# Gathered tokens of experts 1 to 15 turned by 32x32 blocks on VectorE, and w_down loaded as whole rows

## The reference, cut to what matters

```python
    tok = h.reshape(T, D)
    logits = (tok @ router_w).astype(jnp.float32)
    aff = jax.nn.softmax(logits, axis=-1)
    cap = max(1, min(T, CAPACITY_FACTOR * T // N_EXPERTS))
    gate, idx = lax.top_k(aff.T, cap)
    xs = tok[idx]
    hid = jax.nn.silu(jnp.einsum('ecd,edf->ecf', xs, w_gate)) * jnp.einsum('ecd,edf->ecf', xs, w_up)
    ye = jnp.einsum('ecf,efd->ecd', hid, w_down) * gate[..., None].astype(h.dtype)
    out = jnp.zeros_like(tok).at[idx.reshape(-1)].add(ye.reshape(-1, D))
```

## Time and profile before

| what | us |
|---|---|
| median of 3 runs (1491.0 to 1491.63) | 1491.59 |
| span of the profiled execution | 1489.4 |
| PE busy | 1467.0 (99%) |
| DVE busy | 1189.5 (80%) |
| ACT busy | 819.8 (55%) |
| POOL busy | 167.3 (11%) |
| slot_tokens_T_lo, 15 times 1024 elements | 18.3 |

### The profile page before, as it was taken

One profiled execution on the slowest core, in us unless ns is written; L12 is line 12 of the kernel. 1 busy time (PEld: TensorE's weight loads), 2 busy tenths in 40 slices (PEclk: granted clock), 3 DMA queues, 4 the chain that ended last, 5 costly groups with the idle time before them and its releaser, 6 DMA issues.

```text
span 1489.4 us, 18913 instructions
## 1 busy us (share of the span) xinstructions
PE 1467.0 (99%) x7042; PEld 1235.5 (83%) x7042; DVE 1189.5 (80%) x1024; ACT 819.8 (55%) x777; POOL 167.3 (11%) x119
## 2 busy tenths in 40 slices
PE   9999999999999999998999999999999999999996
PEld 8878888888888888888888888888888888888885
DVE  5688988896767766346888888888888888888886
ACT  6322232123622222333677777777777777777776
POOL 1000001000005200011110112011110121012101
PEclk9999999999999999999999999999999999999998
DMA  7210232623263255677999999999999999999997
GB/s 236 58 43 0 81 87 75 224 85 99 94 230 121 87 183 197 227 253 283 347 362 365 376 376 374 384 374 377 374 377 381 377 374 374 384 376 376 374 374 286
DMA packets 220971, 388.26 MB, mean 261 GB/s; under 512 B 8603, under 2 KB 87771, under 8 KB 220412
## 3 DMA queue, kind: packets, MB, share of 16 engines
q1 hardware_dynamic: 213692, 361.39, 68.4%
q0 software_dynamic: 7232, 26.22, 5.8%
HBM read 348.78 MB, written 38.80 MB: 260 GB/s over the span
## 4 chain that ended last, share of the span: by engine, by line
PE 71%; DVE 2%; DMA 0%; issue 0%; ACT 0%; POOLq 0%; POOL 0%; ACTq 0%
PE ps L1779 23%; PE ps L1781 22%; PE ps L1780 22%; PE ps L2162 1%; PE ps L2154 1%; PE ps L2199 1%; PE ps L2082 0%; PE ps L2064 0%; DMA slot_tokens<-tok_rows,rows_to_gather 0%; DVE top_index L1651 0%; DVE affinity_rows L1654 0%; DVE top_of_halves L1647 0%; DVE expert_lo L1207 0%; DVE tok_rows L1592 0%; ACT expert_hi L804 0%
## 5 line engine op out<-in xcount | busy, mean ns | idle before, releaser
L1207 DVE TENSOR_TENSOR expert_lo<-expert_raw,expert_hi 128x2048 fp32r<-128x2048 f32 (+1 forms) x285 | 597.5, 2110 | 92.1 <-ACT expert_hi L804 91.1
L804 ACT ACTIVATE expert_hi<-expert_raw 128x2048 fp32r<-128x2048 f32 (+1 forms) x285 | 506.5, 1778 | 177.8 <-PE ps L1781 174.0
L1779 PE MATMUL ps<-expert_hi,slot_tokens_T_hi 128*128 128x512 f32 (+1 forms) x768 | 289.8, 377 | 2.0 <-DVE slot_tokens_T_lo L1207 1.0
L1780 PE MATMUL ps<-expert_lo,slot_tokens_T_hi 128*128 128x512 f32 (+1 forms) x768 | 285.2, 371 | 0.0
L1781 PE MATMUL ps<-expert_hi,slot_tokens_T_lo 128*128 128x512 f32 (+1 forms) x768 | 285.2, 371 | 0.0
L1779 PE MATMUL ps<-hT_hi,w_hi 128*128 128x512 f32 x576 | 226.2, 393 | 1.0 <-DVE hT_lo L1219 1.0
L1781 PE MATMUL ps<-hT_hi,w_lo 128*128 128x512 f32 x576 | 224.3, 389 | 0.0
L1780 PE MATMUL ps<-hT_lo,w_hi 128*128 128x512 f32 x576 | 224.2, 389 | 0.0
L1779 PEld LDWEIGHTS ps<-expert_hi,slot_tokens_T_hi 128*128 128x128 f32 x768 | 144.1, 188 | 25.1 <-issue 4.0
L1781 PEld LDWEIGHTS ps<-expert_hi,slot_tokens_T_lo 128*128 128x128 f32 x768 | 144.2, 188 | 20.4
L1241 DVE SCALAR_TENSOR_TENSOR conv_sum<-a_padded,small_params,conv_sum 128x1024 f32<-128x1024 f32 x120 | 158.1, 1317 | 3.4
(11 more groups left out here) (314 smaller groups left out, 1843.6 us busy)
## 6 DMA issues: line engine op xcount, KB each, us to landing
expert_raw<-in_w_gate SPq DMA_DIRECT2D x64, 1024.0 KB, 8.7
expert_raw<-in_w_up SPq DMA_DIRECT2D x64, 1024.0 KB, 8.6
expert_raw<-in_w_down SPq DMA_DIRECT2D x64, 1024.0 KB, 8.1
expert_raw<-in_w_gate SPq DMA_DIRECT2D x32, 768.0 KB, 7.5
expert_raw<-in_w_up SPq DMA_DIRECT2D x32, 768.0 KB, 7.2
expert_raw<-in_w_down SPq DMA_DIRECT2D x32, 768.0 KB, 8.5
w_raw<-in_w_in SPq DMA_DIRECT2D x36, 512.0 KB, 4.8
gate_in<-gate_spill SPq DMA_DIRECT2D x22, 512.0 KB, 3.9
```

What stands on the lines that cost most here:

```text
L804: nc.scalar.activation(out, src, ACT.Copy, **scale).then_inc(s, 1)
L1207: V.tensor_tensor(out, src, high_part.bitcast(F32), ALU.subtract).then_inc(s, 1)
L1779: nc.tensor.matmul(out, a[0], b[0], start=first, stop=False)
L1780: nc.tensor.matmul(out, a[0], b[1], start=False, stop=False)
```

## The change

**Tokens.** For experts 1 to 15 the 8 transposes on PE are gone. POOL copies four numbers a partition (`pieces_to_gather`) and issues four indirect DMAs, each of 128 pieces of 1 KB: of a token row's four quarters, the one that a partition gets depends on the 32-partition group that it lies in, and on which of the four DMAs it is. DVE then turns XS in place in blocks of 32x32 (`turn_tokens`, one STREAM_TRANSPOSE over 8x128 elements a partition, seen with a step of 8 elements, 32 bytes), right behind the low part of block 12. After it partition p holds, of each token, the channels 8p to 8p+7. So gate and up weights are loaded with 8 adjoining rows to a partition ("(p t)" for "(t p)"), in pieces as long as before. `xsT_high` and `xsT_low` read XS in SBUF with a step of 32 bytes, where they read PSUM with none, and write as before. The gather for expert e+1 is now issued ahead of the scatter of expert e-1, once `xsT_low` of expert e is done. On PE `hidden_T(2)` follows block 17 without a wait, and the wait for `xsT_lo` is behind it. XS of expert 0 is still turned by PE.

**Start.** The numbers of the pieces are made once: four small ACT copies (`slots_four_times`), four small PE transposes (`slot_pieces`), one DVE tensor_scalar and four memsets.

**w_down.** A block is two row tiles of all 1024 columns (pieces of 4 KB in DRAM), where it was all row tiles of 512 columns (2 KB). For chunks 0 and 1 that is 2048 elements as before; for chunk 2 it is 2048 elements and 1024 in place of twice 1536. PE goes through both column halves of a tile before the next tile, and ACT's scaling of the output waits for both blocks.

```diff
@@ -417,16 +423,20 @@
             if kind == "down":
-                tiles = n // P
-                return w_down[bass.ds(e, 1), a:a + n, k * 512:(k + 1) * 512].rearrange(
-                    "o (t p) n -> p (o t) n", p=P), tiles, 512
+                tiles, _ = place_of(kind, c, k)
+                a += 2 * k * P
+                return w_down[bass.ds(e, 1), a:a + tiles * P, :].rearrange("o (t p) n -> p (o t) n", p=P), tiles, D
             w = w_gate if kind == "gate" else w_up
-            return w[bass.ds(e, 1), k * 4 * P:(k + 1) * 4 * P, a:a + n].rearrange(
-                "o (t p) n -> p (o t) n", p=P), 4, n
+            return w[bass.ds(e, 1), :, a:a + n].rearrange(
+                "o (p t) n -> p (o t) n", p=P)[:, 4 * k:4 * k + 4, :], 4, n
 
         def place_of(kind, c, k):
             a, n = FC[c]
-            return (n // P, 512) if kind == "down" else (4, n)
+            return (min(2, n // P - 2 * k), D) if kind == "down" else (4, n)
@@ -740,20 +749,20 @@
             def gather(e):
 
-                if not isinstance(e, int):
-                    pool.wait_ge(xs_in, e * 16)
-                    pool.wait_ge(xsT_mm, e)
-                pool.wait_ge(slots_ready, 2)
-                nc.gpsimd.tensor_copy(NEXT_ROWS[:], SLOTS[:, bass.ds(e, 1)]).then_inc(rows_next, 1)
+                pool.wait_ge(xs_in, (e - 1) * 64 + 16)
+                pool.wait_ge(xsT_lo, e)
+                pool.wait_ge(slots_ready, 5)
+                nc.gpsimd.tensor_copy(NEXT_PIECES[:], PIECES[:, bass.ds(e, 1), :].rearrange("p o a -> p (o a)")).then_inc(rows_next, 1)
 
                 pool.wait_ge(x2_mm, WO_DONE)
                 pool.wait_ge(rows_next, e)
-                pool.indirect_dma_start(XS[:], None, tok_dram,
-                                        bass.IndirectOffsetOnAxis(ap=NEXT_ROWS[:], axis=0)).then_inc(xs_in, 16)
+                for a in range(4):
+                    pool.indirect_dma_start(XS[:, a * 256:(a + 1) * 256], None, tok_pieces,
+                                            bass.IndirectOffsetOnAxis(ap=NEXT_PIECES[:, a:a + 1], axis=0)).then_inc(xs_in, 16)
@@ -772,16 +781,19 @@
             gather(1)
+            gather(2)
             scatter(0)
-            with pool.Fori(1, E - 1) as e:
+            with pool.Fori(2, E - 1) as e:
                 gather(e + 1)
-                scatter(e)
+                scatter(e - 1)
+            scatter(E - 2)
@@ -1108,17 +1120,18 @@
-                act.wait_ge(xsT_mm, e + 1)
-                high(XST[0][:].rearrange("p k n -> p (k n)"), PS[:, 6:8, :].rearrange("p a n -> p (a n)"), xsT_hi)
+                act.wait_ge(xs_turned, e + 1)
+                act.wait_ge(e_used, e * NB - SKIPPED - len(down_units(1)))
+                high(XST[0][:], XS_BY_TILE, xsT_hi)
 
             def gate_out(e, used):
 
                 for dh in range(2):
                     act.wait_ge(slots_ready, 3)
-                    act.wait_ge(e_used, used + dh)
+                    act.wait_ge(e_used, used + 1)
@@ -1132,6 +1145,12 @@
+                    if first and n == 2:
+                        act.wait_ge(pair_ready, 1)
+                        for a in range(4):
+                            part = nc.scalar.activation(FOUR_TIMES[:, a, :, :], PAIR[:, 1, 32 * a:32 * a + 32][:, None, :].to_broadcast([E, 4, P // 4]),
+                                                        ACT.Copy)
+                        part.then_inc(rows_ready, 1)
@@ -1704,17 +1724,25 @@
+                    dve.wait_ge(slots_mm, 3)
+                    V.tensor_scalar(PIECES[:].rearrange("p e a -> p a e"), PS[:, 4, 0:4 * E].rearrange("p (a e) -> p a e", a=4),
+                                    4.0, QUARTER[:], ALU.mult, ALU.add).then_inc(slots_ready, 1)
                     return
                 dve.wait_ge(xsT_hi, e + 1)
-                low(XST[1][:].rearrange("p k n -> p (k n)"), PS[:, 6:8, :].rearrange("p a n -> p (a n)"),
-                    XST[0][:].rearrange("p k n -> p (k n)"), xsT_lo)
+                low(XST[1][:], XS_BY_TILE, XST[0][:], xsT_lo)
+
+            def turn_tokens(e):
+                dve.wait_ge(xs_in, e * 64 + 16)
+                V.transpose(XS_BY_TILE, XS_BY_TILE).then_inc(xs_turned, 1)
+
+            TURN_AT = 12
 
             def dve_body(e, base, first, last=False):
@@ -2222,14 +2264,18 @@
                 else:
-                    tokens_of(e + 1)
                     down(1, e, down_counts(1, e, base))
+                    hidden_T(2, e)
                     pe.wait_ge(xsT_lo, e + 2)
-                    hidden_T(2, e)
 
             keep_busy(22)
+            slot_pieces()
```

More of the change, by code:

```diff
@@ L1087, in split_e @@
                 q = pos_mod(n, e, SPLITS)
[L1088 removed]
+                high(block_of(ES[q], *BODY[n]), block_of(EW[r], *BODY[n]), e_hi)
             def silu(c, e, base):
@@ L1567, in _ @@
                 steps.did(V.memset(HALF_START[32 * g:32 * g + 32, :], float(H * g)))
+                steps.did(V.memset(QUARTER[32 * g:32 * g + 32, :], float(g)))
             def row_scale(t):
@@ L1732, in dve_body @@
                         hidden(1, e, base)
+                    if n == TURN_AT and not last:
+                        turn_tokens(e + 1)
                     if n == 14:
@@ L2148, in _, with slot_pieces @@
             nc.tensor.transpose(PS[:, 0, 0:E], PAIR[:, 0, :], IDENT[0:E, 0:E]).then_inc(slots_mm, 1)
+            def slot_pieces():
+                pe.wait_ge(rows_ready, 6)
+                for a in range(4):
+                    mm = nc.tensor.transpose(PS[:, 4, a * E:(a + 1) * E], FOUR_TIMES[:, a, :, :].rearrange("e b n -> e (b n)"),
+                                             IDENT[0:E, 0:E])
+                mm.then_inc(slots_mm, 1)
             def tokens_of(e):
@@ L2187, in down, with landed, down_whole @@
                     ge(pe, ye_ready, e)
-                for dh in halves:
-                    count, q, r = counts[dh]
+                for pair in pairs:
+                    count, q, r = counts[pair]
                     pe.wait_ge(e_lo, count + 1)
-                    for t in range(tiles):
-                        mm = product(PS[:, 4 + dh, :], (HIDT[0][:, t, :], HIDT[1][:, t, :]),
-                                     (ES[q][:, t, :], EL[r][:, t, :]), c == 0 and t == 0, c == NF - 1 and t == tiles - 1)
+                    high_part, low_part = block_of(ES[q], "down", c, pair), block_of(EL[r], "down", c, pair)
+                    for t in range(place_of("down", c, pair)[0]):
+                        tile = 2 * pair + t
+                        for dh in range(2):
+                            cols = slice(dh * 512, (dh + 1) * 512)
+                            mm = product(PS[:, 4 + dh, :], (HIDT[0][:, tile, :], HIDT[1][:, tile, :]),
+                                         (high_part[:, t, cols], low_part[:, t, cols]), c == 0 and tile == 0, c == NF - 1 and tile == last_tile)
                     mm.then_inc(e_used, 1)
-            def down_whole(hidden, tiles, dh, count, stop):
+            def landed(count):
                 pe.wait_ge(e_landed[count % RAWS], 16 * (count // RAWS + 1))
-                for t in range(tiles):
-                    mm = nc.tensor.matmul(PS[:, 4 + dh, :], hidden[:, t, :], EW[count % RAWS][:, t, :],
-                                          start=False, stop=stop and t == tiles - 1)
-                mm.then_inc(e_used, 1)
+            def down_whole(hidden, tile, dh, count, c, pair, stop):
+                rows = block_of(EW[count % RAWS], "down", c, pair)[:, tile % 2, dh * 512:(dh + 1) * 512]
+                return nc.tensor.matmul(PS[:, 4 + dh, :], hidden[:, tile, :], rows, start=False, stop=stop)
             def down_counts(c, e, base):
@@ L2239, in _ @@
             pe.wait_ge(hidT_hi, NF * E + 1)
+            end_tiles = (F - 2 * 512) // P
+            for pair in range(2):
+                landed(E * NB - SKIPPED + pair)
             for dh in range(2):
-                down_whole(HIDT_END, (F - 2 * 512) // P, dh, E * NB - SKIPPED + dh, True)
+                for tile in range(end_tiles):
+                    mm = down_whole(HIDT_END, tile, dh, E * NB - SKIPPED + tile // 2, NF - 1, tile // 2, tile == end_tiles - 1)
+                mm.then_inc(e_used, 1)
 def kernel(**inputs):
```

55 lines of the change are left out of this document (34 added, 21 removed).

## The result

The changed kernel takes 1506.22 us (median of 4 runs, 1505.53 to 1507.35), against 1491.61 for the kernel before on the same chip: a ratio of 1.0098, interval 1.0084 to 1.0113. It is slower by 1%, and the forecast of 1485.6 was on the wrong side; the range of 1483 to 1507 holds the time just inside its upper end. The profiled execution has a span of 1503.7 us, 14.3 more than before.

The account below looks back on a forecast made before the run. PE was taken as the bound, busy for 99% of the span. Seams gain 15 x 0.40 = 6.0 us, other terms 0: span 1489.4 - 6.0 = 1483.4, plus 2.2 for the runs' median gives 1485.6; range 1483 to 1507.

Parts of the forecast that it names:

- the tokens' parts from SBUF: DVE's `xsT_low` at the end of a body: reading with a 32-byte step still takes 1.22 us, costing 0 us.
- my two bounds: For `xsT_low` with the step: no price from below, from `plus_sum`'s 1218 ns; 2.44 us from above.
- The first rival: A new 16 bytes at every element doubles DVE's time: `xsT_low` 2.44, +13.2 to +15.8 us, 1504.8 to 1507.4; chance 0.25.
- its turn's 2.6: DVE's turn behind block 12's low part: at 2.44 us it makes block 13 0.17 late, 15 x 0.17 = 2.6 us.
- The wait at the seam: PE's wait for `xsT_lo` at a body's end: low part done T0+6.46, gate and up T0+6.72 to T0+6.86, gain 0.40.
- T0: Start of the last product of block 15 in a body, 1035.42 in the kernel before; seam times count from it.
- ten spare us in the body: The gather lands some 28 us into the body, the turn comes at 37.7: ten us spare, 0 us cost.
- PE's transposes: Eight per seam ahead of w_down, 0.80 to 0.9 by PE alone; block 16's low part limits w_down's start to 0.39 earlier.
- Block 7: Chunk-2 w_down block, split after block 4's 12 products: ready 1013.2, wanted about 1013.3; 0 us, up to 3 us if off.
- The w_down blocks: Loads of an expert's w_down in 4 KB rows: at most 0.9 us gained; DMA side 0 us.
- the lead: Loads running ahead of use, 36.35 us shrinking to 20.80; PE faster by 0.40 takes 5.9 more; loads don't bind, 0 us.

Follow-up runs that it names:

- the two versions without the step at the seam: Changed kernel with token rows reordered in DRAM so all reads are packed, 1495.36 us; changed kernel with the turn written packed into the output buffer, 1494.75 us.
- a fourth: The version with the tokens' parts in halves, with DVE making block 16's low part in two instructions, one per row tile: 1479.97 us, ratio 0.9919.

## Why the prediction was wrong

**The step that failed** is that of the tokens' parts from SBUF: "I take 1.22, 0 us". It was taken from the lower bound, no price, with an upper one of 2.44 beside it, and measured 2.08: 0.87 us at each of 15 seams, where PE waits for it. The row I leaned on, `plus_sum`, has a step of 2, and the runs show that 2 is the last free step: 1.22 at 2, 1.54 at 3, 2.00 at 4 and 8. The row could not tell between my two bounds, I said so, and still let it decide. The Trainium skill, "SBUF — State Buffer", the note on cachelines under Door 1: The DMA port swizzle, speaks of two hits in 16 bytes for full bandwidth; the steps of 2 and of 8 agree with that, and for the step of 4, which it calls free, the measured 2.00 decides against it. My own sum took a step of 8 to be free as well, and the subtract's 2.00 for 1.22 decides against that.

**The first rival** is the mechanism that came true, with its point of decision at 1.62. Its sum, 1504.8 to 1507.4, holds the measured 1506.22 in part by luck. Its low part was too long (2.44 for 2.08, worth 5.4), its wait behind the low part too short (0.39 for 0.60, worth 3.2), its turn's 2.6 didn't come (the turn took 2.22, about the 2.15 that I called free; by my own rows that cover was 2.19; and from gate and up to the next T0 a body takes 40.6 as before), and 3.3 us of POOL's end were in no case of mine.

**The wait at the seam** was mis-sized as well: 0.13 and a branch of up to 0.27 from the low part's end to gate and up, where 0.60 was measured. In the kernel before, the transposes of `hidden_T(2)` stood between wait and branch and covered most of this: from the low part's end to gate and up it took 0.73 with them. With the right size the change gains 0.13 x 15 = 2 us with free reads, less than the 3.3 of POOL's end: 1491.6 - 2.0 + 3.3 = 1492.9, not 1485.6; the two versions without the step at the seam gave 1495.36 and 1494.75, with first T0s 1.8 and 1.7 later than the kernel before. So there are two reasons for the wrong sign, and the stride alone is not all of it.

**POOL's end.** I had four DMAs in place of one hidden behind ten spare us in the body, which held. The start cost nothing in the changed kernel (gate and up of expert 0 start at 712.17 for 712.56); in the versions that share it they start between 711.72 and 714.91, so that a microsecond or two of the start stays open. What was left out is that the indirect DMAs cost at the end of the kernel, 0.07 us for each of the 45 more.

**What held.** PE's transposes weren't worth 0.80 to 0.9 but what the next late thing left: w_down at T0+0.51 (0.58 forecast). DVE's times stay fixed to T0 to 0.01 us. Block 7 was in time. The w_down blocks take at least 0.84 off the loads of a body (at most 0.9 forecast), and in the changed kernel, whose bodies are longer, the lead didn't bind: it was still 35.3 us at block 284, where the kernel before had 20.80. That w_down alone is worth nothing was right only for this PE: 9 us hang on it once bodies take 46.93.

## What to carry to other kernels

Before data is laid out with a step (the distance from one element to the next in a partition), ask which instruction reads it in the place that somebody waits for, and let the one that lies beside other work pay: the same 2 us turn cost nothing behind block 12, and 0.87 us more of a split cost 0.74 a body at the seam. Work taken from the busiest engine is worth only the distance to the next late thing; here it took three more edits (packed reads at the seam, the wait moved past the loop's branch, the parts made in halves) to turn a loss of 1% into a gain of 0.6%, and a fourth for 0.8%. A part of a change that measures as nothing may be what holds the rest up: test it again beside the faster version.

## What the hardware showed that was not expected

- On DVE, 1024 fp32 elements with a step of 4 or 8: a subtract 2.00 us for 1.22 (one strided operand or two, input or output), a transpose in 32x32 blocks 2.01 for 1.25, but a copy 1.08 for 0.69 (a tensor_scalar and a rounding copy 1.08 too; packed they were not timed). A step of 2 is free for the subtract, 1.22. On ACT a copy takes 2.05 for 1.06.
- With the wait directly ahead of its loop's branch, PE took 0.60 us from the event to the next product, with the wait behind the branch 0.24. A taken branch lasts 0.21 us there, one not taken 0.08.
- POOL's DRAIN at the end took 9.66 us in a kernel with 81 indirect DMAs and 6.39 in one with 36: 0.07 us for each of the 45, of 128 pieces each.
